# A routing table of 16,384 experts by 384 tokens: one-hot products, or zeros and adding indirect DMAs

## The chip, the cores and the metric

The kernel runs on one core of a Trainium2 chip. The time is device microseconds of one execution. The core has five engines that run side by side: PE (TensorE, matmuls), DVE (VectorE), ACT (ScalarE), POOL (GpSimd) and SP (SyncE, which here only issues DMAs). ACT and POOL issue DMAs as well, each on a queue of its own; 16 DMA engines carry out what the queues hold.

## What is computed

The program runs two transformer blocks on one sequence of 512 tokens in float32. The change touches one part of it, the PEER layer of the first block:

```python
def peer(xn, wq, subkeys, u_tab, v_tab):
    q = (xn @ wq).reshape(bsz, s, PEER_HEADS, 2, PEER_HALF)
    sub = jnp.einsum('bshpd,hpnd->bshpn', q, subkeys)
    s_top, i_top = lax.top_k(sub, PEER_TOPK)
    cand = (s_top[..., 0, :, None] + s_top[..., 1, None, :]).reshape(..., PEER_TOPK * PEER_TOPK)
    cand_idx = (i_top[..., 0, :, None] * N_KEYS + i_top[..., 1, None, :]).reshape(...)
    best, pos = lax.top_k(cand, PEER_TOPK)
    expert = jnp.take_along_axis(cand_idx, pos, axis=-1)
    gate = jax.nn.softmax(best, axis=-1)
    ...
    a = gelu(einsum('td,ted->te', xb, u_tab[expert]))
    y = einsum('te,ted->td', gate * a, v_tab[expert])
```

Each token picks 16 experts in each of 8 heads, 128 of the 128 x 128 = 16,384 experts, with a gate for each. Two heads may pick the same expert; their gates then add up.

## The kernel before

Instead of fetching 128 rows of `u` for each token, the kernel multiplies all 16,384 experts with all tokens, and masks the result with a table of gates that is zero nearly everywhere. The first 128 tokens are the exception in the last step: for them the rows of `v` are gathered (SPARSE = 128), and the table covers the other 384 tokens (DENSE). Work goes through three stretches, one after the other, each a block at whose end all engines wait for each other.

**Search** (`route_tokens`, profile 479 to 795 us). A stream of 128 panels of `u` (128 experts by 1024, 512 KB each) runs on PE over this stretch (56 panels) and the next (72). For each panel SP loads it into a ring of four, ACT casts it to a high part (`high_part`, L603), POOL subtracts to get the low part (`low`, L617), PE makes three products of 8 x 128 columns (L59 to L61), ACT applies gelu (L612), and SP stores 128 x 512 results to `hidden` in DRAM. ACT casts two panels ahead of PE. Beside it DVE searches the best experts of four tiles of 128 tokens, one after the other (`top16`, `finish`). PE turns the results (row key, column key and gate) with three transposes per tile into `packed` (`turn`, L1944). For tile 0 DVE also lists addresses (`list_chosen`), which ACT copies to `chosen` during the third tile.

**Table** (`build_routing`, 795 to 1278 us). The other 72 panels. After each of the first 48 panels the engines build the table for 8 tokens: DVE compares the key numbers with 0..127 for row and column (16 instructions, L2141 and L2143), PE multiplies the hot vectors of each token (L2162), ACT copies the result out of PSUM (L2178), and after each six such steps writes 3 MB of table to DRAM (L2183). POOL makes the low parts here too. At the end `load_ahead` on SP loads the first panels of `v`, of the table (`cb_route`) and of `hidden` for the next stretch; the last four stores of `hidden` stand behind that on SP. `Ahead.scalar` and `Ahead.vector` make the first operands of the next stretch from them.

**Combine** (`combine_experts`, 1278 to 1815 us). For 128 panels of `v`: DVE multiplies `hidden` with the table (`cb_prod`, L2335), ACT and DVE split both operands in high and low parts, and PE adds up the products of 384 tokens (`cb_y`). Beside it POOL issues 256 indirect DMAs for tile 0: 128 that gather one 4-byte value on each of 128 partitions (`cb_units_of`, L2380) and 128 that gather rows of 4 KB (`cb_rows`, L2385).

The table in DRAM has the shape `[8, 128, 128, 48]`: blocks of 48 tokens, row key, column key, token. A load of four columns (`routing_of`) is 768 KB in pieces of 768 bytes.

Of the kernel before, what the change touches and what calls it, by code (L numbers as in the profile page):

```python
# [23 lines left out]
TOKENS = DENSE // 8  # L24
# [187 lines left out]
def in_blocks(x):  # L212

    return x.rearrange("p (b t) -> p b t", t=TOKENS)


def routing_of(routing, column, count):

    return routing[:, :, bass.ds(column, count), :].rearrange("b r c t -> r b (c t)")
# [1657 lines left out]
EARLY_CHUNKS = (56, 72)  # L1877


def route_tokens(nc, stream, units, qT, keys, keys_landed, iota, packed, chosen, parted):  # L1880
# [4 lines left out]
    with ExitStack() as ctx:  # L1885
# [16 lines left out]
        token = c.sb("rt_token", [P, 1])  # L1902
# [3 lines left out]
        out_ps = c.ps("rt_out", [P, SEQ])  # L1906
# [3 lines left out]
        EXPS_AT, TURN_AT = share // 4, share * 2 // 3  # L1910
        S = {x: c.sem(f"rt_{x}") for x in ("const", "scored", "copied", "searched", "seq", "shifted",
                                           "exped", "resulted", "turned", "stored", "listed")}
        with nc.Block() as block:
# [7 lines left out]
            def _(pool):  # L1921
# [7 lines left out]
                pool.iota(token[:], pattern=[[0, 1]], base=0, channel_multiplier=1,  # L1929
                          allow_small_or_imprecise_dtypes=True).then_inc(S["const"], 1)  # L1930
                for n in range(units + 2):
                    stream.low(pool, 0, n)

            @block.tensor
            def _(pe):
# [3 lines left out]
                def turn(t):  # L1939
                    pe.wait_ge(S["resulted"], t + 1)  # L1940
                    if t >= 1:
                        pe.wait_ge(S["stored"], t)
                    for i in range(3):
                        last = pe.transpose(out_ps[:, i * P:(i + 1) * P],  # L1944
                                            result[:, i].rearrange("p h k -> p (h k)"), ident[:])
                    last.then_inc(S["turned"], 1)

                def score(t):
                    for i in range(HALVES):
                        if i % 4 == 0 and t >= 1:  # L1950
                            pe.wait_ge(S["copied"], 4 * (t - 1) + i // 4 + 1)
                        last = pe.matmul(banks[i // 4][:, (i % 4) * P:(i % 4 + 1) * P],
                                         qT[:, i, t * P:(t + 1) * P], keys[:, i, :], start=True, stop=True)
# [5 lines left out]
                for t in range(TILES):  # L1959
                    if t + 1 < TILES:  # L1960
                        score(t + 1)
                    for n in range(share):
                        if t >= 1 and n == TURN_AT:
                            turn(t - 1)
                        if t == TILES - 1 and n == share - 1:
                            turn(t)
                        stream.tensor(pe, 0, t * share + n)

            @block.scalar
            def _(act):  # L1970
# [13 lines left out]
                stream.start_high(act)  # L1984
                for t in range(TILES):
# [16 lines left out]
            def _(dve):  # L2002
# [45 lines left out]
                for t in range(TILES):  # L2048
# [23 lines left out]
                    if t >= 1:  # L2072
                        keep(t - 1)
# [1549 lines left out]
```

## Time and profile before

| | us |
|---|---|
| median of 3 runs | 2941.22 |
| lowest and highest | 2936.93, 2941.53 |
| the profiled execution's own time | 2941.4 |
| its span, first to last instruction | 2939.6 |
| search stretch, 479.0 to 795.3 | 316.3 |
| table stretch, 795.3 to 1278.4 | 483.1 |
| combine stretch, 1278.4 to 1815 | 536.6 |

The profile's times count from the first instruction; 1.8 us lie around the span. A row of a timeline is one instruction with its start, its length, its line and its operands, and in brackets how long its engine had been idle and what ended the wait. A matmul's row is as long as the matmul is under way; since the next one starts before it ends, the distance of two starts tells PE's pace, and the busy time does not.

### The profile page before, as it was taken

Reading aid. Unit: us, or ns where it says so; the run is one execution under the profiler, and the core shown is the slowest. Engines: PE = TensorE matmul, PEld = TensorE weight load, DVE = VectorE, ACT = ScalarE, POOL = GpSimd, SP = SyncE. Lnnn points to the kernel's source line nnn. Section 1 sums busy time; section 2 is a strip of 40 time slices with the busy share of each in tenths; the row PEclk is TensorE's granted clock in tenths of the full one; section 3 lists DMA queues with packets and bytes.
Section 4 is the critical chain, followed back from the end, with each engine's and each line's share of the span. In section 5 each row is a group of like instructions: output and inputs, shape, how many; then the busy total and the mean of one; then the engine's idle time right before and its main releaser. Section 6 shows DMA issues by size and latency. Waiting matters only on the chain. (4 is left out here: it accounts for less than half of the span.)

```text
span 2939.6 us, 40172 instructions
## 1 busy us (share of the span) xinstructions
PE 2867.9 (98%) x14214; PEld 2458.4 (84%) x14214; DVE 1781.4 (61%) x3712; ACT 1052.6 (36%) x1499; POOL 799.9 (27%) x509
## 2 busy tenths in 40 slices
PE   8999999999999999999999999999999999999998
PEld 6776878888788888899999998888877787788887
DVE  6586466677687773048888886544244676454432
ACT  4334332333344444233333334332231336333322
POOL 0121202444433333457667650000020230000000
PEclk9999999999999999999999999999999999999999
DMA  4222333444445545479999993323343100233321
GB/s 155 77 93 75 130 108 108 136 140 148 135 151 193 193 152 206 146 286 382 357 357 361 347 372 123 108 93 94 100 122 100 39 30 1 87 100 98 96 98 68
DMA packets 181722, 453.05 MB, mean 154 GB/s; under 512 B 25554, under 2 KB 79442, under 8 KB 180435
## 3 DMA queue, kind: packets, MB, share of 16 engines
q1 hardware_dynamic: 157762, 358.73, 36.5%
q0 software_dynamic: 22528, 67.19, 5.9%
q10 hardware_dynamic: 1296, 25.36, 2.1%
q8 instruction: 80, 1.31, 0.2%
q14 instruction: 56, 0.45, 0.0%
HBM read 386.01 MB, written 65.01 MB: 153 GB/s over the span
## 5 line engine op out<-in xcount | busy, mean ns | idle before, releaser
L59 PE MATMUL cb_y<-cb_g_hi,s_hi 128*128 128x384 f32 x1024 | 342.9, 335 | 2.2 <-DVEq L2326 2.2
L61 PE MATMUL cb_y<-cb_g_hi,s_lo 128*128 128x384 f32 x1024 | 342.8, 335 | 0.0
L60 PE MATMUL cb_y<-cb_g_lo,s_hi 128*128 128x384 f32 x1024 | 342.7, 335 | 0.0
L617 POOL TENSOR_TENSOR s_lo<-ex_raw,s_hi 128x1024 fp32r<-128x1024 f32 x96 | 242.2, 2525 | 345.5 <-ACT s_hi L603 345.5
L59 PE MATMUL bs_ps<-x_hi,s_hi 128*128 128x512 f32 x576 | 229.8, 399 | 2.7 <-PEq L45 2.7
L61 PE MATMUL bs_ps<-x_hi,s_lo 128*128 128x512 f32 x576 | 225.0, 391 | 0.0
L60 PE MATMUL bs_ps<-x_lo,s_hi 128*128 128x512 f32 x576 | 224.8, 390 | 0.0
L2385 POOL DMA_INDIRECT cb_rows<-in_peer_v,ex_chosen x128 | 186.1, 1454 | 68.9 <-issue 37.0
L59 PEld LDWEIGHTS cb_y<-cb_g_hi,s_hi 128*128 128x128 f32 x1024 | 192.8, 188 | 2.6 <-DVEq L2326 2.6
L60 PEld LDWEIGHTS cb_y<-cb_g_lo,s_hi 128*128 128x128 f32 x1024 | 192.7, 188 | 0.0
L61 PEld LDWEIGHTS cb_y<-cb_g_hi,s_lo 128*128 128x128 f32 x1024 | 192.6, 188 | 0.0
L2143 DVE TENSOR_SCALAR br_col<-ex_iota,br_slot 128x128 f32<-128x128 f32 x384 | 191.2, 498 | 0.0
L2306 ACT CAST s_hi<-ex_raw 128x1024 fp32r<-128x1024 f32 x95 | 99.9, 1052 | 231.1 <-PE cb_y L61 207.5
L2141 DVE TENSOR_SCALAR br_row<-ex_iota,br_slot 128x128 f32<-128x128 f32 x384 | 135.0, 351 | 71.1 <-PE br_bank L2162 71.0
L2380 POOL DMA_INDIRECT cb_units_of<-hidden,ex_chosen x128 | 149.9, 1171 | 97.7 <-DVE cb_total L2348 77.4
L59 PE MATMUL rs_ps<-x_hi,s_hi 128*128 128x512 f32 x448 | 174.9, 390 | 0.5 <-POOL s_lo L617 0.5
L61 PE MATMUL rs_ps<-x_hi,s_lo 128*128 128x512 f32 x448 | 174.3, 389 | 0.0
L60 PE MATMUL rs_ps<-x_lo,s_hi 128*128 128x512 f32 x448 | 174.3, 389 | 0.0
L2348 DVE SCALAR_TENSOR_TENSOR cb_total<-cb_rows,cb_weight,cb_total 128x1024 f32<-128x1024 f32 x127 | 162.4, 1279 | 5.2 <-DMA cb_rows<-in_peer_v,ex_chosen 3.7
L2339 DVE TENSOR_TENSOR s_lo<-ex_raw,s_hi 128x1024 fp32r<-128x1024 f32 x95 | 116.3, 1224 | 63.7 <-ACT s_hi L2306 35.0
L291 DVE TENSOR_TENSOR x_lo<-ffn_raw,x_hi 128x1024 fp32r<-128x1024 f32 x63 | 77.1, 1225 | 124.4 <-ACT x_hi L283 124.3
L291 DVE TENSOR_TENSOR ffn_lo<-ffn_raw,ffn_hi 128x1024 fp32r<-128x1024 f32 x63 | 77.1, 1225 | 123.0 <-ACT ffn_hi L283 123.0
(595 smaller groups left out, 6971.6 us busy)
## 6 DMA issues: line engine op xcount, KB each, us to landing
ex_raw<-in_peer_u SPq DMA_DIRECT2D x96, 512.0 KB, 3.5
ex_raw<-in_peer_v SPq DMA_DIRECT2D x96, 512.0 KB
ffn_raw<-in_gu SPq DMA_DIRECT2D x82, 512.0 KB, 3.5
hidden<-up_out SPq DMA_DIRECT2D x128, 256.0 KB, 2.1
routing<-br_out ACTq DMA_DIRECT2D x8, 3072.0 KB, 9.2
cb_route<-routing SPq DMA_DIRECT2D x32, 768.0 KB
cb_unit<-hidden SPq DMA_DIRECT2D x128, 192.0 KB
ffn_raw<-in_down SPq DMA_DIRECT2D x42, 512.0 KB, 3.5
```

The costliest lines, as they stand in the source:

```text
L59: pe.matmul(out, w_high, x_high, start=first, stop=False, skip_group_check=skip)
L60: pe.matmul(out, w_high, x_low, start=False, stop=False, skip_group_check=skip)
L61: return pe.matmul(out, w_low, x_high, start=False, stop=last, skip_group_check=skip)
L291: dve.tensor_tensor(lo[:, k % R, :], raw_of(k), hi[:, k % R, :].bitcast(F32), ALU.subtract).then_inc(split, 1)
L617: eng.tensor_tensor(self.lo[:, s, :], self.raw[s], self.hi[:, s, :].bitcast(F32), ALU.subtract).then_inc(self.split, 1)
L2141: dve.tensor_scalar(row_hot[:, k, b, :], iota[:], slot[:, k, 0, b:b + 1], slot[:, k, 2, b:b + 1], ALU.is_equal, ALU.mult)
L2143: last = dve.tensor_scalar(col_hot[:, k, b, :], iota[:], slot[:, k, 1, b:b + 1], None, ALU.is_equal)
L2306: act.copy(b_hi[:, j, :], b_raw[j]).then_inc(b_high, 1)
L2339: dve.tensor_tensor(b_lo[:, j, :], b_raw[j], b_hi[:, j, :].bitcast(F32), ALU.subtract).then_inc(b_split, 1)
L2348: done = dve.scalar_tensor_tensor(total[:], rows[:, n % V, :], weight[:, n:n + 1], total[:], ALU.mult, ALU.add)
L2380: pool.indirect_dma_start(units_of[:, n:n + 1], None, flat, bass.IndirectOffsetOnAxis(chosen[:, 1, n:n + 1], 0)).then_inc(units_landed[n / ...
L2385: pool.indirect_dma_start(rows[:, n % V, :], None, table, bass.IndirectOffsetOnAxis(chosen[:, 0, n:n + 1], 0)).then_inc(rows_landed[n % V] ...
```

## The change

The table now is `[128, 128, 384]`, one run of 384 tokens for each expert, and it is filled in another way.

- **Zeros.** ACT issues eight transfers of 3 MB (`Scatter.clear`), one ahead of each of the first eight panels of the search stretch. Their source is one row of 512 zeros per partition, repeated, so each piece is 2 KB: 128 x 12 pieces a transfer.
- **Adds.** After the search of a tile DVE computes 128 addresses per token (`list_places`), `(row * 128 + col) * 384 + token`. For each of the 128 slots POOL issues one indirect DMA that adds 128 gates, one of each token of the tile, to the table (`Scatter.add`). That makes 3 x 128 = 384 of them. Within a DMA all places differ; two slots of the same token may hit the same place only in different heads, so a tile's DMAs go in groups of 16 (one head) and each group waits for the one before it of the same tile. 64 stand in the search stretch, two behind each low part of POOL from panel 24 to 55; 320 in the next stretch, in groups of 16 that take turns between the tiles.
- **Order of tiles.** The search goes through tiles 1, 2, 3, 0 instead of 0 to 3. So the list of tile 0 (`chosen`) is there only at the end, and its copy stands at the end of ACT's stretch, with SP waiting for it.
- **Table stretch** (`project_rest` in place of `build_routing`). The hot vectors, their products, copies and table writes are gone, and so are PE's transposes. The low parts of its 72 panels are made by DVE instead of POOL.
- **End of the stretch.** SP waits for all adds (`wait_all`) before it loads the first part of the table; that load now stands last, ahead of the last four stores of `hidden`.

```diff
+    def clear(self, act, zeros, part):
+        ...
+        act.dma_start(to.rearrange("i (r z) -> i r z", z=size),
+                      zeros.unsqueeze(1).broadcast_to([P, rows * DENSE // size, size])).then_inc(self.zeroed, 16)
+
+    def add(self, pool, tile, slot):
+
+        if slot == 0:
+            pool.wait_ge(self.listed, tile + 1)
+        if tile == 0 and slot == 0:
+            pool.wait_ge(self.zeroed, 16 * ZERO_PARTS)
+        if slot and slot % PEER_TOPK == 0:
+            pool.wait_ge(self.added[tile], 16 * slot)
+        pool.indirect_dma_start(self.flat, bass.IndirectOffsetOnAxis(self.place[:, tile, slot:slot + 1], 0),
+                                self.gate[:, tile, slot:slot + 1], None, compute_op=ALU.add
+                                ).then_inc(self.added[tile], 16)
 ...
                 for n in range(units + 2):
                     stream.low(pool, 0, n)
+                    for tile, slot in early.get(n, ()):
+                        scatter.add(pool, tile, slot)
 ...
-                        if t == 2 and n == TURN_AT:
-                            act.wait_ge(S["listed"], 3)
-                            ...
+                        if t == 0 and n < ZERO_PARTS:
+                            scatter.clear(act, zeros[:], n)
                         if t == TILES - 1 and n == share - 3:
                             exps(t)
                         stream.scalar(act, 0, t * share + n, ends=t == TILES - 1)
+                act.wait_ge(S["listed"], 3)
+                ...
 ...
-def build_routing(nc, stream, done, iota, packed, routing, load_ahead, ahead):
+def project_rest(nc, stream, done, scatter, late, load_ahead, ahead):
 ...
+            @block.gpsimd
+            def _(pool):
+                for tile, slot in late:
+                    scatter.add(pool, tile, slot)
 ...
+            @block.vector
+            def _(dve):
+                for k in range(done + 2, stream.n):
+                    stream.low(dve, 0, k)
+                ahead.vector(dve, stream)
 ...
-            sp.dma_start(ahead.route[:, 0], routing_of(routing, 0, RING)).then_inc(ahead.r_landed[0], 16)
             stream.wait_stored(sp, RING)
             for k in range(RING):
                 sp.dma_start(ahead.unit[:, k, :], hidden[k, :, SPARSE:]).then_inc(ahead.h_landed[k], 16)
+            scatter.wait_all(sp)
+            sp.dma_start(ahead.route[:, 0], routing_of(routing, 0, RING)).then_inc(ahead.r_landed[0], 16)
```

On ACT, early in the search stretch, before: casts of the stream's panels (`s_hi`) and gelus (`up_out`) take turns.

```order
L603 CAST s_hi<-ex_raw 128x1024
L612 ACTIVATE up_out<-rs_ps 128x512
L603 CAST s_hi<-ex_raw 128x1024
L612 ACTIVATE up_out<-rs_ps 128x512
L603 CAST s_hi<-first_raw 128x1024
```

The same place after the change:

```order
L1893 DMA routing<-rt_zeros 128x12x512
L597 CAST s_hi<-ex_raw 128x1024
L606 ACTIVATE up_out<-rs_ps 128x512
L1893 DMA routing<-rt_zeros 128x12x512
L597 CAST s_hi<-first_raw 128x1024
L606 ACTIVATE up_out<-rs_ps 128x512
```

A zeroing transfer now stands ahead of each of eight casts.

On POOL, where the search stretch ends and the table stretch begins (the two branches), after the change, with the semaphores that each row waits for:

```order
L611 TENSOR_TENSOR s_lo<-first_raw,s_hi 128x1024 [waits up_high]
L1904 DMA routing<-sc_gate,sc_place 6291456x1 x2
L611 TENSOR_TENSOR s_lo<-ex_raw,s_hi 128x1024 [waits up_high] x2
L1947 UNCONDITIONAL_BRANCH
L2135 UNCONDITIONAL_BRANCH [waits barrier_Pool_Activation_PE_DVE_SP_gather]
L1904 DMA routing<-sc_gate,sc_place 6291456x1 [waits sc_added0]
L1904 DMA routing<-sc_gate,sc_place 6291456x1 x15
L1904 DMA routing<-sc_gate,sc_place 6291456x1 [waits sc_listed]
L1904 DMA routing<-sc_gate,sc_place 6291456x1 x15
```

Before, low parts stood on both sides of the branches; now POOL has nothing but adds behind them, 320 in a row, every sixteenth with a wait.

On SP at the end of the table stretch, before:

```order
L2484 DMA first_raw<-in_peer_v 128x1024 [waits up_split]
L2485 DMA cb_route<-routing 128x8x192
L2488 DMA cb_unit<-hidden 128x384 [waits up_stored1,up_stored0]
L2488 DMA cb_unit<-hidden 128x384 x3
L564 DMA hidden<-up_out 128x512 [waits up_active] x4
```

And after:

```order
L2460 DMA first_raw<-in_peer_v 128x1024 [waits up_split]
L2463 DMA cb_unit<-hidden 128x384 [waits up_stored1,up_stored0]
L2463 DMA cb_unit<-hidden 128x384 x3
L2465 DMA cb_route<-routing 128x1536 [waits sc_added2,sc_added1,sc_added0]
L558 DMA hidden<-up_out 128x512 [waits up_active] x4
```

The load of the table moved behind the loads of `hidden` and waits for the three tiles' adds; the four stores stand behind it as before.

## Rows read from the trace of the kernel before

**Rows 1.** Busy us (instructions) of PE, PEld, DVE, ACT, POOL; PEclk, DMA share, GB/s; by stretch.

```profile
479.00:795.30 316.30, 313.57 (x1420) 260.51 (x1420) 225.89 (x821) 104.07 (x135) 151.69 (x57) 1.00 0.42 141
795.30:1278.40 483.10, 480.86 (x2497) 411.25 (x2497) 273.00 (x819) 206.61 (x241) 170.07 (x70) 1.00 0.49 173
1278.40:1815.00 536.60, 536.11 (x3088) 535.78 (x3088) 433.48 (x532) 190.04 (x258) 339.29 (x260) 1.00 0.92 338
```

**Rows 2.** Timeline (start us, us) of PE: two hot-vector blocks, then panels without them.

```profile
802.44 1.95 PE L2162 MATMUL br_bank<-br_col,br_row 128*128 128x128 f32 x16
...
809.70 1.95 PE L2162 MATMUL br_bank<-br_col,br_row 128*128 128x128 f32 x16
...
1145.36 0.48 PE L59 MATMUL bs_ps<-x_hi,s_hi 128*128 128x512 f32 x1
...
1275.81 0.39 PE L61 MATMUL bs_ps<-x_hi,s_lo 128*128 128x512 f32 x1
1278.40 0.41 PE L59 MATMUL cb_y<-cb_g_hi,s_hi 128*128 128x384 f32 x1 [2.20 <-DVEq L2326]
```

**Rows 3.** Timeline of POOL in the search stretch: low parts, one free and one contested.

```profile
604.25 2.39 POOL L617 TENSOR_TENSOR s_lo<-ex_raw,s_hi 128x1024 fp32r<-128x1024 f32 x1 [3.05 <-ACT s_hi L603]
609.70 3.79 POOL L617 TENSOR_TENSOR s_lo<-ex_raw,s_hi 128x1024 fp32r<-128x1024 f32 x1 [3.06 <-ACT s_hi L603]
```

**Rows 4.** Timeline of ACT at the end of the search stretch.

```profile
792.65 0.60 ACT L612 ACTIVATE up_out<-rs_ps 128x512 f32<-128x512 f32 x1 [4.27 <-PE rs_ps L61]
795.25 1.05 ACT L603 CAST s_hi<-ex_raw 128x1024 fp32r<-128x1024 f32 x1 [2.00 <-PEq L45]
```

**Rows 5.** Page, DMA issues: out, in, queue, count, KB each, us to landing.

```profile
hidden<-up_out SPq DMA_DIRECT2D x128, 256.0 KB, 2.1
routing<-br_out ACTq DMA_DIRECT2D x8, 3072.0 KB, 9.2
```

**Rows 6.** Timeline of SP in the combining stretch: a long issue.

```profile
1286.11 8.06 SPq L2286 DMA_DIRECT2D cb_unit<-hidden  x1
```

**Rows 7.** DMA over 1278.4 to 1286.1: queue with packets, MB, share; and issues.

```profile
q1 hardware_dynamic: 1294, 1.41, 51.8%
...
cb_route<-routing SPq DMA_DIRECT2D x2, 768.0 KB
ex_raw<-in_peer_v SPq DMA_DIRECT2D x3, 512.0 KB
cb_unit<-hidden SPq DMA_DIRECT2D x4, 192.0 KB
first_raw<-in_peer_v SPq DMA_DIRECT2D x1, 512.0 KB
```

**Rows 8.** Timeline of POOL in the combining stretch: gathers, free and contested.

```profile
1285.84 0.94 POOL L2380 DMA_INDIRECT cb_units_of<-hidden,ex_chosen  x1 [0.31 <-issue]
...
1289.59 1.25 POOL L2380 DMA_INDIRECT cb_units_of<-hidden,ex_chosen  x1 [0.30 <-issue]
...
1294.88 1.60 POOL L2380 DMA_INDIRECT cb_units_of<-hidden,ex_chosen  x1 [0.30 <-issue]
...
1323.71 1.36 POOL L2380 DMA_INDIRECT cb_units_of<-hidden,ex_chosen  x1 [0.30 <-issue]
1325.38 1.30 POOL L2385 DMA_INDIRECT cb_rows<-in_peer_v,ex_chosen  x1 [0.30 <-issue]
```

**Rows 9.** Timeline of DVE beside them.

```profile
1288.79 1.22 DVE L2339 TENSOR_TENSOR s_lo<-ex_raw,s_hi 128x1024 fp32r<-128x1024 f32 x1 [3.14 <-issue]
...
1300.62 0.17 DVE L2357 TENSOR_TENSOR cb_weight<-cb_units_of,ex_chosen 128x8 f32<-128x8 f32 x1 [2.07 <-DMA cb_units_of<-hidden,ex_chosen]
```

**Rows 10.** Busy time of the engines in the contested stretch.

```profile
1305.70:1340.00 34.30, 34.30 (x200) 34.30 (x199) 31.27 (x40) 13.93 (x19) 28.20 (x21) 1.00 1.03 385
```

**Rows 11.** DMA queues over 1298 to 1305, with 4-byte gathers alone on q0.

```profile
q0 software_dynamic: 154, 0.00, 1.6%
```

**Rows 12.** Timeline of ACT at the end of the table stretch.

```profile
1273.61 0.60 ACT L612 ACTIVATE up_out<-bs_ps 128x512 f32<-128x512 f32 x1 [7.66 <-DMA hidden<-up_out]
```

More of the change, by code:

```diff
@@ L23 @@
 DENSE = SEQ - SPARSE
-TOKENS = DENSE // 8
 class Chip:
@@ L1937, in _ @@
                 pe.wait_ge(S["const"], 2)
[L1939 to L1946, printed above, removed]
                 def score(t):
@@ L1999, in _ @@
                         stream.scalar(act, 0, t * share + n, ends=t == TILES - 1)
+                act.wait_ge(S["listed"], 3)
+                each = SPARSE * SLOTS // P
+                for part in range(P // SPARSE):
+                    act.dma_start(chosen[part * SPARSE:(part + 1) * SPARSE],
+                                  listed[:, :, part * each:(part + 1) * each]).then_inc(parted, 16)
             @block.vector
@@ L2149, in _ @@
-            @block.gpsimd
-            def _(pool):
-                for k in range(done + 2, stream.n):
-                    stream.low(pool, 0, k)
-            @block.tensor
-            def _(pe):
-                pe.sem_inc(S["product"], 2)
-                def body(it, o, step, n, k):
-                    pe.wait_ge(S["hots"], n + 1 + 2)
-                    pe.wait_ge(S["taken"], n + 1)
-                    for b in range(B):
-                        last = pe.matmul(banks[2 * k + b // 4][:, b % 4, :], row_hot[:, k, b, :],
-                                         col_hot[:, k, b, :], start=True, stop=True)
-                    last.then_inc(S["product"], 1)
-                both(pe, body, lambda g, k, ends: stream.tensor(pe, g, k))
@@ L2194, in _ @@
             @block.sync
             def _(sp):
-                groups = stream.n // RING
                 stream.sync_groups(sp, FROM, groups - 1)
-                for o in range(2):
-                    sp.wait_ge(stored[o], 16 + 16 * (n_blocks // 2))
                 load_ahead(sp)
@@ L2445, in combine_experts, with scatter_order, experts @@
     clear_semaphores(nc, [*ahead.sems, *stream.sems, parted, *sparse, *named], no_gpsimd_drain=True)
-def experts(nc, first, gains, hT, x_hi, x_lo, s_hi, s_lo, d, routing, hidden, gathered, plain, then_plain):
+def scatter_order(units):
+    tiles = DENSE // P
+    begin = units // TILES + 10
+    early = {n: [divmod(EARLY_EACH * (n - begin) + i, SLOTS) for i in range(EARLY_EACH)] for n in range(begin, units)}
+    left = [list(range(SLOTS)) for _ in range(tiles)]
+    for pairs in early.values():
+        for tile, slot in pairs:
+            left[tile].remove(slot)
+    late = []
+    while any(left):
+        for tile in range(tiles):
+            size = len(left[tile]) % PEER_TOPK or PEER_TOPK
+            late += [(tile, slot) for slot in left[tile][:size]]
+            left[tile] = left[tile][size:]
+    return early, late
+def experts(nc, first, gains, hT, x_hi, x_lo, s_hi, s_lo, d, routing, hidden, gathered, scattered, plain, then_plain):
     searching = EARLY_CHUNKS[0]
@@ L2473, in experts @@
                                  load_keys_and_units, ring=own_ring)
-            route_tokens(nc, stream, searching, qT, keys, keys_landed, iota, packed, chosen, parted)
+            early, late = scatter_order(searching)
+            route_tokens(nc, stream, searching, qT, keys, keys_landed, iota, scatter, early, chosen, parted)
         ahead = Ahead(c)
@@ L3480, in build_program @@
         gathered = [c.sem(f"cb_gathered{i}") for i in range(6)]
+        scattered = [c.sem(f"sc_added{i}") for i in range(DENSE // P)]
         primed, prime = c.sb("primed", [P, 1]), c.sem("primed")
```

174 lines of the change are left out of this document (65 added, 109 removed).

## The prediction

> **What bounds the kernel now.** I read the busy times by stretch first. In the table stretch PE is busy 480.9 of 483.1 us, in the search stretch 313.6 of 316.3, in the combine stretch 536.1 of 536.6 [rows 1]. The reader should see that every stretch that the change touches ends when PE ends, and that DVE, ACT and POOL have room: 57%, 43% and 35% in the table stretch. So only two kinds of edit count: PE's work, and what newly comes later than PE. The clock is granted in full in all three rows. Then I read PE's timeline for its pace [rows 2]. Two hot-vector blocks start 7.26 us apart (802.44 and 809.70). After the last one, 24 panels of the stream run from 1145.36 to 1276.04 (the last start plus the 0.23 us by which matmuls follow each other), 5.445 us each. The difference, 1.82 us per step at this place, is the price of a hot-vector block on PE. Last I read the other queues for what would now carry the table: POOL's indirect DMAs, SP's long issue, and the end of the table stretch.
>
> **PE loses its hot-vector work.** Before, PE needs 1276.04 - 795.3 = 480.7 us for 72 panels and 48 blocks. After, it needs 72 x 5.445 = 392.0, plus 1.4 us of slow start that the stretch has now too, 393.4. On PE this saves 87.3 us. DVE's 768 comparisons, ACT's 96 copies and eight table writes go as well; they lay beside PE and give nothing. The 12 transposes in the search stretch go too: they are passes of the size of the 16 in a hot-vector block, 12/16 of 1.82 us, and the first matmul behind each of four breaks is longer by 0.1 (0.48 for 0.39 [rows 2]), 1.8 us. Total on PE: 89 us. This is the whole possible gain.
>
> **The end of the search stretch.** The copy of `chosen` now is issued behind ACT's last gelu, and SP waits for it. Today that gelu ends at 793.25 and the next stretch begins 2.0 us later [rows 4]. A small transfer needs about as long to land as the 256 KB store, 2.1 us [rows 5]; I add 2.3 us. DVE has its list by then: it loses its waits for the transposes and its result of the last tile was ready at about 783.
>
> **The zeros on ACT.** The eight transfers hold 25 MB, as much as the table writes that go, and a 3 MB write lands in 9.2 us [rows 5]. But they are cut finer: 128 x 12 = 1536 pieces of 2 KB. SP shows what many pieces do to a queue. Between 1278.9 and 1285.8 it issued two loads of the table (1024 pieces each) and eight plain loads (128 each), 3072 pieces; 1294 had moved by 1286.1 [rows 7], so some 1780 were outstanding, and the next issue held SP for 8.06 us [rows 6]. If ACT's queue does the same, transfer number 8 is accepted when all but 1780 of the 12,288 pieces are through: 6.84 transfers of 9.2 us, 63 us after the first. PE's pace would have had ACT there after 7 x 5.445 = 38 us. ACT is 25 us late; it casts two panels ahead, and of the 10.9 us that this gives, the gelu and cast (0.60 and 1.05 [rows 4], with their starts about 2.0) and the low part (2.39 [rows 3]) leave 6.5 us. PE then loses 18 us. Below, the bound is 0 (ACT's queue takes them all); above, 31 us, if a transfer takes 11 us beside the stream's loads. I take 18, from the row that is nearest.
>
> **Adds in the search stretch.** POOL's low part takes 2.39 us and it then idles 3.05 of each panel [rows 3]. Two adds at 1.25 us (0.94 and 0.31 idle, as the gathers show [rows 8]) fit into 3.05. Where DVE works long on two operands, a low part takes 3.79 [rows 3], and adds will stretch too, but the two-panel lead covers one such burst of some 5 us. Cost taken: 0, at most 8 us (32 panels, 0.25 us each, if an add costs 1.65).
>
> **Adds in the table stretch.** This is the term that decides. 320 adds stand in a row on POOL, and SP, the first table load and the next stretch wait for the last. No row shows an adding DMA. The nearest are the gathers of 4 bytes on 128 partitions: 0.94 + 0.31 = 1.25 us from start to start when DVE is silent [rows 8]. Beside a DVE low part (1288.79 to 1290.01 [rows 9]) one took 1.25 instead of 0.94 [rows 8], 0.31 more. With DVE busy 31.3 of 34.3 us [rows 10], starts are 1.67 us apart [rows 8]. After the change DVE makes one such low part per 5.445 us, four adds long, so 0.31 / 4.1 = 0.08 more per add: 1.33 us, and 320 x 1.33 = 426 us. Bounds: 1.25 (400 us) and 1.67 (534 us). The DMA engines are no limit if adds are like gathers: in a stretch where only such gathers ran on their queue, they took 1.6% of 16 engines [rows 11]. The waits in groups of 16 cost nothing at this pace: two tiles taking turns leave 21 us for a landing that takes 4.1 us (the last gather of eight ends at 1296.48 [rows 8], DVE gets them at 1300.6 [rows 9]).
>
> What the Trainium skill says on this I keep apart: in "SBUF — State Buffer", section "SBUF: two separate sides", VectorE and GpSimd share a port pair as an exclusive lock, and GpSimd cannot write a DMA's descriptors while it is out. This speaks against putting the low parts on DVE beside a row of indirect DMAs. By that rule an add waits for all of a low part; the result is the fourth rival. Of the rule, the trace bears out that there is a cost, and not its size.
>
> **The end.** From the last add's landing on: SP issues the table load and the store of panel 124, each 0.4; ACT's gelu of 126 waits for that store, as it does today for 7.66 us [rows 12], then come cast, DVE's low part of 1.2 us and the split of the first product, then the block's end, 1.6 us. In sum about 8 us. Loads of `v` and `hidden` have long landed.
>
> **The sum.** The search stretch's last gelu begins at 792.65 - 1.8 + 18 = 808.9; POOL begins its adds at 795.3 - 1.8 + 18 + 2.3 = 813.8. It ends at 1239.4, the last add has landed at 1243.5, the combine stretch starts at 1251.5. PE alone would be ready at 813.8 + 393.4 + 2.4 = 1209.6, so it now idles 42 us: POOL has become the bound. Today the stretch starts at 1278.4 [rows 2]; 26.9 us are gained. Nothing behind it changes: PE sets its pace there, and the table's coarser pieces (6 KB for 768 bytes) only ease the DMAs, which are 92% busy but not waited for. The profiled execution took 2941.4 us (span 2939.6 and 1.8 around it), the median is 2941.2: **2914.5 us**.
>
> **Rivals.**
> *ACT's queue takes the zeros.* The 18 us are not lost, all else stays: 2896. For it: the long row is SP's, in another stretch, and only one. Against: it is the only row on a full queue.
> *Best case.* In addition adds run at 1.25: the combine stretch begins at 796 + 400 + 12 = 1208, 2871 us; PE's 1191.6 is the floor, at 2855.
> *Adds cost POOL more than gathers: slower than before.* An add has to name its source, the place to read and the place to write, where a gather names two. Its place is the row of 320. With the 18 us, gain turns to loss when (1278.4 - 12.1 - 813.8) / 320 = 1.414 us per add are passed, without them at 1.47. At the contested pace of 1.67 it is 320 x 0.34 = 109 us more: 3023; at 1.6, 3001. For it: nothing shows an add, and the limit is only 0.08 above my value. Against: rows of 4 KB and of 4 bytes cost alike [rows 8], so cost goes by the number of pieces, which is 128 here too.
> *POOL stands still for the whole of each low part on DVE.* 72 x 1.22 = 88 us instead of some 26, 2977, slower too. Against: the one gather beside such a low part lost 0.31 [rows 8], and with DVE busy 91% [rows 10] POOL still issued one every 1.67 us.
> *The DMA engines are slow on adds.* If the additions of a DMA ran without overlap, each would take its landing time, 4.1 us: 320 x 4.1 = 1312 us, some 3800 in total. It decides from 1.41 us per DMA on the engines. The 1.6% of the gathers [rows 11] speaks against it; a read that a write depends on is in no row.
>
> **How the numbers follow.** Forecast (queue blocks, adds at 1.28 to 1.41) 0.34; no block 0.26; best case 0.08; costly adds 0.21; a full stand-still of POOL 0.04; slow engines 0.05; the rest, a gain and a cost that cancel, 0.02. The first three give 0.68, of which 0.04 come near enough to 2941 to be no change. A measurement of this kernel tells 0.2%, 6 us, from nothing. Faster 0.63, within 0.2% 0.06, slower 0.31. The range reaches from the best case to the contested adds at 1.6, 2868 to 3005; the forecast's own, by 0 and 31 us of block and 1.28 to 1.41 us, is 2880 to 2953.
>
> **What would show it.** A table stretch without hot-vector blocks, and with PE idle at its end for some 40 us: POOL is the bound; with panels 5.445 apart, that part is right. Starts of adds on POOL 1.25 to 1.4 us apart confirm the term; over 1.5, the third rival; idle time on POOL ended by a DMA at every sixteenth, the last. Issues of the zeros on ACT of some 8 us and low parts 9 us apart around 490 to 550 confirm the block; issues of 0.4 us refute it. The prediction is wrong if the first table load is issued far from 1244 us, or if the combine stretch is not 536.6 us long.

## The result, and the profile after

The changed kernel took **3121.7 us** (median of 4 runs, 3115.1 to 3130.4) against 2939.5 of the kernel before on the same chip: a ratio of 1.062, 95% interval 1.060 to 1.065. It is 182 us slower. The prediction was 2914.5 us, 27 us faster; its range ended at 3005. The profiled execution took 3123.9 us (span 3122.2). All ratios leave out one run of the kernel before that took 3604 us, where its other runs lay between 2937 and 2947.

First the busy times by stretch of the changed kernel: length, then busy us (instructions) of PE, PEld, DVE, ACT, POOL, PEclk, DMA share, GB/s. The stretches are the search, the part of the table stretch in which PE works, its wait, and the combining. In every fence below, "..." marks what is left out.

```profile
478.10:839.50 361.40, 326.25 (x1408) 261.17 (x1408) 231.77 (x828) 103.91 (x135) 253.42 (x121) 0.98 0.61 193
839.50:1233.40 393.90, 393.88 (x1726) 325.98 (x1727) 86.03 (x70) 107.38 (x140) 330.19 (x208) 0.99 0.65 144
1233.40:1452.40 219.00, 0.67 (x3) 0.21 (x3) 2.25 (x3) 2.55 (x5) 173.35 (x112) 0.51 0.25 9
1452.40:1995.00 542.60, 538.19 (x3088) 535.81 (x3088) 435.05 (x533) 189.92 (x258) 339.67 (x260) 1.00 0.91 335
```

Beside [rows 1]: the search is 45.1 us longer (361.4 for 316.3). The table stretch is 612.9 us instead of 483.1, 129.8 more, although PE's own part fell from 480.7 to some 394. The combining is 6.0 longer. Some 3 us are spread behind it. The 219 us in the third row are the case: PE idles (the granted clock falls to 0.51, the level of 1.2 GHz), the DMAs carry 9 GB/s, and only POOL works.

The page names what PE waited for (line, engine, instruction, count | busy us, mean ns | idle before <- what ended it), and what the new DMAs cost:

```profile
L1904 POOL DMA_INDIRECT routing<-sc_gate,sc_place x384 | 611.1, 1591 | 117.8 <-issue 112.0
L58 PE MATMUL cb_y<-cb_g_hi,s_hi 128*128 128x384 f32 x1024 | 343.1, 335 | 218.9 <-DVEq L2282 218.4
L58 PE MATMUL rs_ps<-x_hi,s_hi 128*128 128x512 f32 x448 | 180.2, 402 | 29.3 <-POOL s_lo L611 29.3
L606 ACT ACTIVATE up_out<-bs_ps 128x512 f32<-128x512 f32 x72 | 43.1, 598 | 501.1 <-DMA hidden<-up_out 224.2
```

One add holds POOL for a mean of 1591 ns and the next follows 0.30 us later. The 384 adds fill 611 us of POOL, and PE's first product of the combining waited 218.4 us. The third row is the second loss: in the search, PE waited 29.3 us for POOL's low parts, where the kernel before waited 0.5. The fourth row is ACT's wait for a store of `hidden`, which SP issues only behind the adds and the load of the table. POOL's timeline (start us, us) in the table stretch:

```profile
1003.68 1.55 POOL L1904 DMA_INDIRECT routing<-sc_gate,sc_place  x1 [0.31 <-issue]
1005.53 1.55 POOL L1904 DMA_INDIRECT routing<-sc_gate,sc_place  x1 [0.30 <-issue]
1007.38 2.46 POOL L1904 DMA_INDIRECT routing<-sc_gate,sc_place  x1 [0.30 <-issue]
1010.14 1.55 POOL L1904 DMA_INDIRECT routing<-sc_gate,sc_place  x1 [0.31 <-issue]
```

Starts are 1.85 us apart; beside the gathers of [rows 8] (0.94, 1.25 from start to start) that is 0.60 more. Every idle time is a bare 0.30 of issue: nothing is waited for. In the whole trace POOL waited for a DMA 1.4 us, once. The third row is what contention looks like here: an add longer by 0.91. DVE's timeline beside it:

```profile
1001.83 1.25 DVE L611 TENSOR_TENSOR s_lo<-first_raw,s_hi 128x1024 fp32r<-128x1024 f32 x1 [4.30 <-ACT s_hi L597]
1007.19 1.23 DVE L611 TENSOR_TENSOR s_lo<-ex_raw,s_hi 128x1024 fp32r<-128x1024 f32 x1 [4.11 <-ACT s_hi L597]
```

The long add began at 1007.38, 0.19 us into a low part that ended at 1008.42. Its extra 0.91 us is what was left of the low part, 1.04, less 0.13. The add of 1001.82 began just ahead of a low part and kept its 1.55. All 208 adds over PE's part fit this: nine began 0.06 to 0.21 us into a low part and took 0.89 to 1.03 us more, and none that began ahead of one was longer. The experiments below show the same: in seven traces 303 of the 304 lengthened DMAs beside DVE's 70 low parts are longer by the rest of the low part less 0.11 to 0.14 us.

In the part with DVE's low parts beside it the mean is 1587 ns, in the part where DVE is silent 1548:

```profile
L1904 POOL DMA_INDIRECT routing<-sc_gate,sc_place x208 | 330.2, 1587 | 67.3 <-issue 63.1 <-POOLq L44 4.2
...
L1904 POOL DMA_INDIRECT routing<-sc_gate,sc_place x111 | 171.8, 1548 | 33.9 <-issue 33.9
```

These are POOL's groups over 839.5 to 1233.4 and over 1236 to 1441. The difference, 0.04 us per add, is 8 us in all: three adds take 5.56 us and a low part comes every 5.445, so here the two rarely met in the bad order.

In the search, POOL's timeline shows a low part and two adds per panel:

```profile
806.33 2.99 POOL L611 TENSOR_TENSOR s_lo<-ex_raw,s_hi 128x1024 fp32r<-128x1024 f32 x1
809.48 1.55 POOL L1904 DMA_INDIRECT routing<-sc_gate,sc_place  x1 [0.17 <-issue]
811.34 1.55 POOL L1904 DMA_INDIRECT routing<-sc_gate,sc_place  x1 [0.30 <-issue]
812.33 2.98 POOL L611 TENSOR_TENSOR s_lo<-ex_raw,s_hi 128x1024 fp32r<-128x1024 f32 x1
```

Low parts start 6.00 us apart, and PE could take one every 5.445. POOL has no idle time left before them, where it had 3.05 in [rows 3].

ACT's timeline at the start of the search holds the zeros; the number behind the start is how long the issue held the queue:

```profile
477.60 0.45 ACTq L1893 DMA_DIRECT2D routing<-rt_zeros  x1
...
489.32 2.77 ACTq L1893 DMA_DIRECT2D routing<-rt_zeros  x1
...
494.76 8.89 ACTq L1893 DMA_DIRECT2D routing<-rt_zeros  x1
...
503.86 9.65 ACTq L1893 DMA_DIRECT2D routing<-rt_zeros  x1
...
533.51 9.64 ACTq L1893 DMA_DIRECT2D routing<-rt_zeros  x1
```

The last issue ends at 543.15, 65.5 us after the first began. The row of [rows 6] was no peculiarity of SP: a second queue does the same. The queue's packets (q10) tell how full it was: up to 543.15 it had moved 9492, and 2924 were still to come.

Last the end of the table stretch, on POOL and then on SP:

```profile
1439.07 1.55 POOL L1904 DMA_INDIRECT routing<-sc_gate,sc_place  x1 [0.31 <-issue]
...
1442.23 0.33 SPq L2465 DMA_DIRECT2D cb_route<-routing  x1
1442.60 8.18 SPq L558 DMA_DIRECT2D hidden<-up_out  x4
```

The last add ends at 1440.62, SP issues the table's first load 1.6 us later, and the combining starts at 1452.4, 11.8 us after the add.

### The profile page after: what moved, and what is told of

The parts are those of the page before. It is cut to its first block and busy times, and to the rows that moved or that the text cites. A ratio compares the mean times of both kernels' runs of the same rounds, so it can differ in the third digit from the quotient of the medians.

```text
span 3122.2 us, 37818 instructions
## 1 busy us (share of the span) xinstructions
PE 2797.4 (90%) x13434; PEld 2375.3 (76%) x13434; DVE 1604.0 (51%) x2974; ACT 956.4 (31%) x1403; POOL 1235.1 (40%) x824
## 3 DMA queue, kind: packets, MB, share of 16 engines
q0 software_dynamic: 77824, 67.41, 10.6%
## 5 line engine op out<-in xcount | busy, mean ns | idle before, releaser
L1904 POOL DMA_INDIRECT routing<-sc_gate,sc_place x384 | 611.1, 1591 | 117.8 <-issue 112.0
L58 PE MATMUL cb_y<-cb_g_hi,s_hi 128*128 128x384 f32 x1024 | 343.1, 335 | 218.9 <-DVEq L2282 218.4
L58 PE MATMUL rs_ps<-x_hi,s_hi 128*128 128x512 f32 x448 | 180.2, 402 | 29.3 <-POOL s_lo L611 29.3
L606 ACT ACTIVATE up_out<-bs_ps 128x512 f32<-128x512 f32 x72 | 43.1, 598 | 501.1 <-DMA hidden<-up_out 224.2
L611 DVE TENSOR_TENSOR s_lo<-ex_raw,s_hi 128x1024 fp32r<-128x1024 f32 x52 | 63.8, 1226 | 230.7 <-ACT s_hi L597 230.7
L611 POOL TENSOR_TENSOR s_lo<-ex_raw,s_hi 128x1024 fp32r<-128x1024 f32 x44 | 126.1, 2882 | 75.0 <-ACT s_hi L597 75.0
L2294 DVE TENSOR_TENSOR s_lo<-ex_raw,s_hi 128x1024 fp32r<-128x1024 f32 x95 | 116.3, 1225 | 69.2 <-ACT s_hi L2262 40.9
```

The costliest lines, as they stand in the source:

```text
L58: pe.matmul(out, w_high, x_high, start=first, stop=False, skip_group_check=skip)
L606: act.activation(self.out[:, s, :], self.ps[s][:], self.function).then_inc(self.active, 1)
L611: eng.tensor_tensor(self.lo[:, s, :], self.raw[s], self.hi[:, s, :].bitcast(F32), ALU.subtract).then_inc(self.split, 1)
L1904: pool.indirect_dma_start(self.flat, bass.IndirectOffsetOnAxis(self.place[:, tile, slot:slot + 1], 0), self.gate[:, tile, slot:slot + 1], ...
L2294: dve.tensor_tensor(b_lo[:, j, :], b_raw[j], b_hi[:, j, :].bitcast(F32), ALU.subtract).then_inc(b_split, 1)
```

## The experiments

**Theory A**: the addition itself costs POOL 0.60 us per DMA, and that alone turned the change around. **Rivals**: POOL is slowed by what is beside it (DVE's low parts, 25 MB of zeros), writing to scattered places costs it, or the DMA queue pushes back. All experiments start from the changed kernel. The kernel before took 2939.5 to 2942.2 us (medians) on the chips used, so their times can be set side by side.

**A plain write instead of an add.** Slots that two heads share keep the last value only.

```diff
-                                self.gate[:, tile, slot:slot + 1], None, compute_op=ALU.add
+                                self.gate[:, tile, slot:slot + 1], None
```

> The changed kernel with one argument less: the 384 indirect DMAs write their gates into the table instead of adding them (the addition is left out; where two heads of a token pick the same expert, the table holds one gate). Places, counts and waits are the same. Theory A, the addition is what costs (three addresses for each piece instead of two): POOL's instruction falls from 1.55 to the gathers' 0.94 us, a start every 1.25 us, the 320 adds take about 407 us instead of 600, search loses its 20 us behind the adds, and the time is about 3122 - 193 - 20 = 2909 us. Theory B, writing at scattered places costs, whether it adds or not: 1.55 us stays, 3122 us. Theory C, contention with VectorE's low parts sets it: 1.55 us stays too.

Measured: 2931.0 us (6 runs), ratio to the kernel before 0.997 (0.996 to 0.998). One keyword in one line is 191 us. The expectation of 2909 was 22 us too low. The timeline of POOL:

```profile
849.72 0.96 POOL L1904 DMA_INDIRECT routing<-sc_gate,sc_place  x1 [0.30 <-issue]
850.99 0.96 POOL L1904 DMA_INDIRECT routing<-sc_gate,sc_place  x1 [0.31 <-issue]
852.25 1.27 POOL L1904 DMA_INDIRECT routing<-sc_gate,sc_place  x1 [0.30 <-issue]
...
857.61 1.43 POOL L1904 DMA_INDIRECT routing<-sc_gate,sc_place  x1 [0.30 <-issue]
```

A plain write costs what a gather costs, 0.96 + 0.30 = 1.26. The same places, tables, zeros and low parts are there, so neither the scattering nor the neighbours are the cause of the 0.59 us. From the first write of the table stretch to the last, 320 take 1.355 us each: the term that the prediction set at 1.33. The third and fourth rows are the part of it that the expectation left out. 70 of 290 writes began under a low part of DVE (here 0.79 and 0.63 us into it) and were longer by what was left of it less some 0.12 us, so the mean beside low parts is 1.05 us, and 320 writes take 434 us where 407 were expected.

**A gather instead of an add** (the table keeps its zeros). The same line, the other way round:

```diff
-        pool.indirect_dma_start(self.flat, bass.IndirectOffsetOnAxis(self.place[:, tile, slot:slot + 1], 0),
-                                self.gate[:, tile, slot:slot + 1], None, compute_op=ALU.add
+        pool.indirect_dma_start(self.got[:, tile, slot:slot + 1], None, self.flat,
+                                bass.IndirectOffsetOnAxis(self.place[:, tile, slot:slot + 1], 0)
```

> The changed kernel with the 384 adding DMAs turned round: each gathers 128 values of 4 bytes from the same places of the table into a scratch tile (the table then stays zero, its filling is left out). Theory A and theory B both expect what the gathers of the kernel before show with VectorE nearly silent: 0.94 us per instruction, a start every 1.25 to 1.28 us, about 2909 us. Theory C (contention in this stretch, the size of the table, the addresses) expects 1.55 us and 3122 us. My forecast had 1.33 us for this form, so this also measures that step by itself: with 1.28 us the 320 take 410 us.

Measured: 2926.2 us (3 runs), ratio 0.995 (0.994 to 0.997), 0.944 us of POOL each (median), with the same lengthening under low parts. Reading and writing differ by 0.014 us. The direction is nothing, the addition all: that an indirect DMA adds, and nothing beside it, makes the 0.59 us. Why it does, the runs do not show.

**Fewer pieces.** Adds of 64 and of 32 partitions, plain writes of 64; the values of the other partitions are left out. The edit is the range of partitions, as here:

```diff
-        pool.indirect_dma_start(self.flat, bass.IndirectOffsetOnAxis(self.place[:, tile, slot:slot + 1], 0),
+        pool.indirect_dma_start(self.flat, bass.IndirectOffsetOnAxis(self.place[:64, tile, slot:slot + 1], 0),
...
```

> The changed kernel with each add on 64 of the 128 partitions (the gates of the other half of the tokens are left out). It tells what part of the 1.55 us goes by the pieces. Theory A1, cost goes by pieces over a fixed part: half the pieces save well over 0.3 us, 0.8 to 1.2 us per instruction; with 1.1 to 1.5 us from start to start the 320 take 350 to 480 us, 2880 to 3000 us in total. Theory A2, the cost is one of the instruction: 1.55 us, 3122 us.

> Edit: the adds for partitions 0 to 31 alone (three quarters of the values are left out of the table). A price that is linear in the pieces (1.25 + 0.15 for every 64) gives 1.32 us of POOL per add; 1.40 as with 64 pieces would say that the lower part is a fixed price, and something near 1.0 that the first step was only the beginning.

> Edit: plain writes instead of adds, as in e1_scatter, and for partitions 0 to 63 alone (half the values are left out of the table). With e6_half (the same for adds: 1.40 us against 1.55) it splits the price of the addition. If the addition's 0.60 us are paid per instruction, half a plain write costs 0.95 - 0.15 = 0.80 us, and the difference to e6_half stays 0.60. If they are paid per piece, a plain write has no cost per piece and stays at 0.95, with 0.45 between the two.

The rows on this tile in the traces of the three, in that order (duration in ns: min/median/max, first and last start):

```profile
L1904 POOL DMA_INDIRECT routing<-sc_gate,sc_place x384: 1397/1401/3757, 631.9 to 1402.7; - x192
```

```profile
L1904 POOL DMA_INDIRECT routing<-sc_gate,sc_place x384: 1302/1302/3682, 629.2 to 1385.3; - x192
```

```profile
L1904 POOL DMA_INDIRECT routing<-sc_gate,sc_place x384: 887/894/3212, 627.6 to 1235.0; - x192
```

Adds of 128, 64 and 32 pieces cost 1.547, 1.401 and 1.302 us; plain writes of 128 and 64 cost 0.958 and 0.894. An add over a write is 0.59 us at 128 pieces and 0.51 at 64. Drawn on as a line through 128 and 64, about 0.4 us of it are paid per instruction and 0.17 for the pieces: neither pure case of the expectations. At 32 pieces the line gives 1.33 us (the expectation had 1.32), a little above the 1.302 measured. A quarter of the pieces still costs 84% of the time, so cutting pieces does not rescue an adding DMA. In the kernel it saves less still: from the first late add to the last, one takes 1.88, 1.77 and 1.74 us, because with the shorter adds, 1.70 and 1.61 apart, nearly every low part has an add that begins under it and waits (69 each beside the 70 low parts, where the full adds had nine). The kernels took 3084.3 (2 runs), 3071.3 and 3283.7 us (one run each). The last number fits neither theory; it has a part of its own below.

**Zeros ahead of every second panel**, so that ACT's queue never fills.

```diff
-                        if t == 0 and n < ZERO_PARTS:
-                            scatter.clear(act, zeros[:], n)
+                        if (t * share + n) % 2 == 0 and (t * share + n) // 2 < ZERO_PARTS:
+                            scatter.clear(act, zeros[:], (t * share + n) // 2)
```

> The changed kernel with the eight zeroing transfers ahead of every second panel (0, 2, ... 14) instead of the first eight: 10.9 us apart, where ACT was held 9.7 us for each from the fourth on. Theory: the loss of some 20 us early in the search stretch goes, since a transfer is through before the next is issued (issues of 0.4 us), and the adds, which begin at panel 24, still find the zeros landed: 3122 - 20 = 3102 us. Rival: the stretch is bound by POOL's low parts and adds anyway and the gain is given back there, or the wait for the zeros moves to POOL at panel 24: 3115 to 3122 us.

**The same, with all adds in the table stretch** (`EARLY_EACH = 0`).

> Edit: zero transfers ahead of every second panel, as in e3_spaced, and no add in the search stretch: all 384 stand in the table stretch. Theory (an add costs POOL 1.85 us, so two of them and a low part, 6.0 us, do not fit in a panel of 5.4): the search stretch loses its last 20 us against e3_spaced's, about 313 us instead of 333; the adds take 384 x 1.878 = 721 us from the end of the search on, the combine stretch starts about 1533 us and the time is about 3203 us, although the search is faster. Rival (the search stretch is still slowed by the zero transfers' own traffic, 25 MB beside the panels): it stays at 330 us, whatever stands on POOL, and the time is 3220.

Measured: 3096.8 us (4 runs), 25 less than the changed kernel (20 expected), and 3194.3 us (2 runs; 3203 expected, with a search of 313 for the 315.5 measured). In the second, the waits of PE over the search and the table stretch (what for, us in total, times, longest) are:

```profile
PE cb_y L58 <- DVEq L2282: 336.9, 1, 336.9
PE bs_ps L58 <- PEq L44: 3.5, 1, 3.5
PE rs_ps L58 <- POOL s_lo L611: 0.5, 1, 0.5
```

With the plain writes as a fourth corner (they are short enough to fit into a panel) the lengths from the first panel of the search to the first of the table stretch form a square:

| | no adds, or short ones | adds of 1.85 us, two per panel |
|---|---|---|
| zeros spaced | 315.5 | 340.1 |
| zeros in a row | 338.9 (plain writes) | 361.4 |

The block by the zeros is worth 21 to 23 us, the early adds 22 to 25, and they add up. The plain writes are only nearly free, so the left column can hold a little of theirs. In both spaced kernels the issues of the zeros took 0.38 to 0.45 us. The search of 315.5 us, with all zeros and no adds, is no longer than the 316.3 of the kernel before, so the transfers' own traffic costs it next to nothing. The late placement loses more than it wins: 64 adds moved back are 120 us on the path, against 25 in the search.

**A mixture.** The runs say that POOL can place a part of the table in the time in which PE does the rest. Two tiles of 128 tokens come by indirect DMAs, the third by hot products as before, with zeros for two tiles and spaced, and head 0's 16 slots by plain writes, since nothing lies there yet. The core of the edit:

```diff
-                                self.gate[:, tile, slot:slot + 1], None, compute_op=ALU.add
+                                self.gate[:, tile, slot:slot + 1], None,
+                                **(dict(compute_op=ALU.add) if slot >= PEER_TOPK else {})
...
+                for n in range(stream.n - done):
+                    stream.tensor(pe, FROM, n)
+                    if n % EACH == EACH - 1 and n // EACH < HOT:
+                        product(n // EACH)
```

> Edit: only two of the three 128-token tiles are written by indirect DMAs (head 0's 16 slots of a tile as plain writes, the other 112 as adds; 32 of them beside the search, one per panel), the third tile by the one-hot products of the kernel before, eight tokens after every fourth panel; zeros for two tiles alone, ahead of every second panel; the table in blocks of 64 tokens. The output is the reference's. Theory (the table stretch ends with the later of PE, 393.9 us of panels + 128 x 0.227 = 423, and POOL, 208 x 1.88 + 16 x 1.26 = 411): 480.7 - 423 = 57 us less in the table stretch than in the kernel before, 9 us more for the add's landing and the late load of the table, so 2890 to 2900 us. Rival (adds beside hot products, low parts and the block stores on one core's DMA queues cost more than 1.88 us each): POOL ends last; at 2.1 us the adds take 457 us and the time is about 2935, no gain.

Measured: 2914.0 us (4 runs), ratio 0.992 (0.990 to 0.993): a gain, but 14 to 24 us less than expected. PE's part took 429.7 us (796.4 to 1226.1; expected 423). POOL's last add ended at 1234.7: from its first late one POOL took 438 us for the 411 expected. The 208 late adds, beside low parts and comparisons, took 1.65 us in the mean instead of 1.58, and POOL stood still for 11 us more than the bare issues, 5.7 of them for the landing of earlier adds. An add so cost 1.95 us from start to start, between the theory's 1.88 and the rival's 2.1. PE waited 21.0 us at the end. So POOL still came last, and the next run takes adds from its end:

```diff
-    early = {n: [divmod(EARLY_EACH * (n - begin) + i, SLOTS) for i in range(EARLY_EACH)] for n in range(begin, units)}
+    counts = [EARLY_EACH + (n >= units - 14) for n in range(begin, units)]
...
```

> Edit: e7_mix with 14 of its late adds moved beside the search: two adds per panel instead of one in the last 14 panels (46 early, 210 late). In e7_mix PE's part of the table stretch ends at 1226 us, the last add is issued at 1233 and the combine stretch starts at 1247. Theory (the later of PE and POOL, plus 12 us from the last add to the combine stretch): the late adds end 14 x 1.87 = 26 us earlier, about 1207, the combine stretch starts right behind PE's last panel and the load of what it needs, 1230 to 1235 us, so 12 to 17 less than e7_mix: 2897 to 2902 us. Rival (two adds and a low part, 6.0 us, in a panel of 5.4 us hold PE up beside the search as they did in the changed kernel): 14 x 0.6 = 8 us come back there, less what the low parts' lead takes up, and the time is about 2907.

Measured: **2901.3 us** (4 runs), ratio 0.986 (0.984 to 0.988): the fastest kernel of this study. PE's waits and the rows of the panels (start of the first and last):

```profile
PE bs_ps L59 <- PEq L45: 7.2, 1, 7.2
PE rs_ps L59 <- POOL s_lo L617: 4.5, 5, 2.1
PE cb_y L59 <- DVEq L2361: 2.5, 1, 2.5
```

```profile
L59 PE MATMUL bs_ps<-x_hi,s_hi x576: 389/389/766, 803.2 to 1227.2; 128*128 128x512 f32 x192
...
L59 PE MATMUL cb_y<-cb_g_hi,s_hi x1024: 334/334/522, 1230.5 to 1766.3; 128*128 128x384 f32 x171
```

The combining starts 2.9 us behind PE's last panel, at 1230.5 (expected 1230 to 1235), 16.6 earlier than in the first mixture. The rival has its share too: the search is 7 us longer (325.0 for 317.9), near the 8 that it named for the 14 adds. The sum of the two lies inside the theory's interval. PE is the bound again.

**Half a plain write, once more.** The run of 3283.7 us asked for a second look at the same kernel.

> Edit: the same kernel as e8_half_write (plain writes of 64 partitions), run once more, because its one run took 3284 us, 352 more than the same writes of all 128 partitions, with PE idle and the other DMAs at a tenth of their rate between 820 and 1240 us. If that belongs to the kernel (64-piece writes issued every 1.2 us starve the other queues), it comes back at about 3280 us. If it was an event of that run, the time is near e1_scatter's, 2915 to 2931 us.

Measured: 3267.9 us (2 runs), on another chip. It belongs to the kernel. But the expectation named the wrong victim: it is not the DMAs that starve first. PE's timeline while the half writes run:

```profile
927.48 0.58 PE L60 MATMUL bs_ps<-x_hi,s_lo 128*128 128x512 f32 x1 [2.22 <-issue]
930.27 0.58 PE L58 MATMUL bs_ps<-x_hi,s_hi 128*128 128x512 f32 x1 [2.22 <-issue]
933.08 0.59 PE L59 MATMUL bs_ps<-x_lo,s_hi 128*128 128x512 f32 x1 [2.22 <-issue]
```

PE has its operands (the idle time is "issue", nothing that a semaphore ends) and starts a matmul only every 2.8 us instead of 0.23. PE's weight loads stand in the middle of these gaps (926.08, 928.88), so every instruction of PE comes 1.40 us behind the one before. The clock is not the reason: it is granted at 0.52, the lower level, from 850 to 1230 us, but a matmul is only 0.2 us longer by it. A panel takes 67 us: some 20 idle, eight matmuls 0.43 us apart or less, then 16 that are 2.8 us apart. The slow pace sets in at 844, 27 us after the first late write, and ends at 1262, 24 us after the last one began. Adds of the same 64 partitions, 1.70 us apart, and full writes, 1.26 apart, do not do this; half writes, 1.195 apart, do. From about 1000 us on these take 1.09 us themselves and come 1.40 apart, the very distance of PE's instructions. Why is open, and no run here takes it apart.

## Why the prediction was wrong

The steps of the prediction against what was measured, in its order:

- *PE's saving*: predicted 393.4 us for its part of the table stretch, measured 394.4 by the same rule (the last start, 1233.68, plus 0.23). Right.
- *The end of the search*: the transposes gone and the copy behind the last result were put at 0.5 us more in sum. The kernel with spaced zeros and no early adds shows 315.5 for 316.3, 0.8 less. Small, as predicted.
- *The zeros*: predicted acceptance of the eighth 63 us after the first and 18 us lost to PE; measured 65.5, and 21 to 23 us by the square above. The mechanism was right, the size 3 to 5 us short. That the 63 us came so near is in part luck, for two numbers in it were off and cancel: 2924 pieces were outstanding at that moment, not 1780, and 1536 pieces took 10.6 us beside the stream's loads (9492 in 65.5 us), not 9.2. The rival of an unblocked queue (chance 0.26) is refuted by five issues of 8.9 to 9.7 us.
- *Early adds*: predicted 0, at most 8; measured 22 to 25. This is a consequence of the next step: two adds at 1.25 fit into POOL's 3.05 us of idle time, two at 1.85 do not. The 0.55 us by which 6.00 exceeds 5.445 make 18 us over 32 panels; the rest is not taken apart. With plain writes of 1.26 the step holds to 2 us (338.9 - 315.5 = 23.4, of which 21.3 are the zeros').
- ***The adds in the table stretch*: the step that failed.** Predicted 1.33 us each and 426 us for 320, with bounds of 1.25 and 1.67. Measured from 839.8 to 1440.6: 600.8 us, 1.878 each. The 0.55 us too little make 175 us. The row for it was a gather's, and the gather is the right row for a write: that is what 1.355 in the plain-write run says. The addition is another 0.59 us on each. No row of before showed an addition, and the upper bound was that of a *contended gather*, not of an *unknown instruction*. The argument against the third rival, that the cost goes by the number of pieces, held between gathers and failed at the new kind: by the line above, most of its surplus does not depend on pieces.
- *Contention by DVE*: predicted 0.08 us per DMA. Measured 0.04 for the adds (8 us in all instead of 26), 0.10 for the plain writes. The mean was a fair guess, the picture behind it was not: an indirect DMA that begins under a low part waits for the rest of it, less some 0.12 us, and one that began ahead of it is not touched. This accounts for the one contested gather that the prediction had: it began at 1289.59 under the low part that ended at 1290.01, 0.42 were left, and it lost 0.31. The fourth rival (88 us, POOL at a standstill for every low part) did not come, since only nine of 208 adds began where they had to wait, and for the rest of a low part only. But its mechanism is there, and the adds got off lightly by their rhythm: with 32 pieces the mean beside low parts is 1.49 us for 1.30 without, with plain writes 1.05 for 0.96. The prediction took the rule in the Trainium skill's "SBUF — State Buffer" ("SBUF: two separate sides") as a wait for all of a low part. The section gives the shared pair, between a VectorE operation with two SBUF inputs and a GpSimd operation that reads SBUF, to whichever starts first, for the whole instruction. For POOL's side the trace agrees: each DMA that began at least 0.06 us into a low part, with more than 0.14 us of it left, waited for its end. For DVE's it does not: low parts that began behind an add kept 1.22 to 1.27 us. The section's sentences on descriptors speak of a VectorE operation in a two-port mode, and no run here shows which access of the DMA it is that waits.
- *DMA engines*: q0 took 10.6% over the span for 5.9% before. No limit, as predicted; that POOL waited 1.4 us for a DMA refutes the fifth rival.
- *The end*: predicted 12.1 us from the last add to the combining, measured 11.8.
- *The combining*: predicted 536.6, measured 542.6. PE is busy 2.1 us longer in it (the clock is at 0.50 over the first 3.6 us behind the wait, and a matmul takes 0.52 us for 0.33), and idles 4.4 us in place of 0.5.

These terms add up: 175 (price of the late adds) + 26 (they start at 839.8 instead of 813.8) - 0.3 (end) + 6.0 (combining) + 2.6 (behind it) = 209.3, against 3123.9 - 2914.5 = 209.4.

The third rival, with a chance of 0.21, was what happened: adds cost POOL more than gathers, in the place and beyond the break-even of 1.414 us per add that it named. Its reason, three addresses for each piece instead of two, is not shown, and a surplus that is mostly paid per instruction speaks against it as the main one. Its price was too low: it went to 1.67, and the range to 1.6. At the measured 1.85 even a perfect placement would have lost: 320 x 1.85 = 592 us on POOL alone against PE's 483.

## What to carry to other kernels

When a change rests on a row of several hundred instructions of a kind that the trace does not show, its price is the forecast: work out the break-even per instruction first, and when the nearest known kind is only 6% below it, as here (1.33 to 1.414), widen the range by the whole price of what the new kind does in addition. An indirect DMA that adds holds the issuing engine 1.6 times as long as one that writes, so write plainly wherever nothing lies yet. And when a second engine can do a job more slowly than the first, split the job so that both end together: all of it on POOL lost 182 us, two thirds of it, with spaced zeros and plain writes for the first head, won 41. A last point is for rows of indirect DMAs beside long two-operand instructions of DVE: which of the two begins first decides whether a DMA waits, so the same low parts cost full adds 0.04 us each and the shortest ones 0.19.

## What the hardware showed that was not expected

- An indirect DMA with an addition: 1.547 us of GpSimd for 128 pieces of 4 bytes, 1.401 for 64, 1.302 for 32; a plain write 0.958 and 0.894, a gather 0.944; between two of them 0.30 always. It moves more packets too: over the kernel q0 has 77824 with adds, 34816 with plain writes and 22528 in the kernel before. That is 144 packets for an add of 128 pieces and 32 for a write. With 64 and 32 pieces an add has 80 and 48 (53248 and 40960 in all), one for each piece and 16 more, while a write of 64 keeps its 32.
- An indirect DMA that begins while DVE is in a low part of 1.23 us (both inputs in SBUF) is longer by the rest of it less some 0.12 us: 0.89 with 1.02 left, 0.70 with 0.83, 0.31 with 0.42. One that begins ahead of the low part keeps its time, and the low part keeps its own, to 0.05 us.
- A full queue holds the engine that issues to it: transfers of 3 MB in 1536 pieces issued from ACT held it for 8.9 to 9.7 us from the fourth on, with some 2900 pieces outstanding when the last was taken, and for 0.38 us when 10.9 us apart. Whether pieces or bytes set the limit, no run separates.
- While plain indirect writes of 64 partitions run, 1.195 us apart at first, TensorE's instructions come 1.40 us apart and its matmuls 2.8. Both traces show it, on two chips, and all three executions took 337 to 353 us more than the full writes. Unexplained.
